# Two joint attention jobs side by side, and the attention's steps written out between the units of the projection

## What is computed

```
h = rmsnorm(x, norm_mix)
proj = h @ w_in                     # 1024 x 5888
qa, ka, va, qb, kb, vb, g_a, g_b = split(proj)
# a: 12 heads of 64 in three groups of four, windows (128,1), (512,4), (2048,16);
#    each head: softmax over its own window, with a slope times the distance
w_grp = softmax(stack(lses), axis=0)            # over the three groups
y_a   = sum(w_grp * outs)                       # 256 wide: four heads' sums over three groups
# b: 8 heads of 64, causal with a slope
merged = sigmoid(g_a) * (y_a @ w_up_a) + sigmoid(g_b) * (y_b @ w_up_b)
x = x + merged @ w_out
```

## Time and profile before

| | |
|---|---|
| median of 3 runs | 1197.73 us (1196.47 to 1199.54) |
| the profiled execution: its own time | 1196.15 us |
| its span, first to last instruction | 1194.3 us |
| PE busy | 1173.3 us (98% of the span) |
| PEld busy | 993.7 us (83%) |
| DVE busy | 810.8 us (68%) |
| ACT busy | 595.6 us (50%) |
| POOL busy | 51.1 us (4%) |
| TensorE's granted clock, mean | 0.999 |
| read from HBM | 251.63 MB, 212 GB/s over the span |

### The profile page before, as it was taken

The page is one execution under the profiler, slowest core; times in us unless marked ns, Lnnn a source line. Parts: engine busy times, 40 slices in busy tenths (PEclk is TensorE's granted clock), DMA queues, the critical chain, the costliest instruction groups (busy, mean ns, idle before and its releaser), DMA issues.

```text
span 1194.3 us, 15399 instructions
## 1 busy us (share of the span) xinstructions
PE 1173.3 (98%) x6300; PEld 993.7 (83%) x6300; DVE 810.8 (68%) x1037; ACT 595.6 (50%) x776; POOL 51.1 (4%) x101
## 2 busy tenths in 40 slices
PE   8999999999999999999999999999999999999998
PEld 6888887999999888888777888888789978888887
DVE  5777876437646658787899876787784657545544
ACT  8443346545563653433568554334465675533431
POOL 0011110000000001111000000111000000000000
PEclk9999999999999999999999999999999999999999
DMA  9888693553334668886725357887636405655540
GB/s 372 337 314 301 238 360 141 181 185 129 106 130 159 242 229 290 298 302 235 281 81 182 133 209 263 312 300 266 244 112 241 159 1 211 221 181 197 176 141 36
DMA packets 44422, 253.68 MB, mean 212 GB/s; under 512 B 5568, under 2 KB 5952, under 8 KB 20544
## 3 DMA queue, kind: packets, MB, share of 16 engines
q1 hardware_dynamic: 29088, 199.78, 46.1%
q0 software_dynamic: 13824, 50.34, 11.9%
q10 hardware_dynamic: 1440, 2.58, 0.6%
HBM read 251.63 MB, written 1.05 MB: 212 GB/s over the span
## 4 chain that ended last, share of the span: by engine, by line
PE 44%; ACT 2%; DVE 2%; DMA 1%; issue 1%; SPq 0%; DVEq 0%; ACTq 0%
PE ps L1767 11%; PE ps L1769 11%; PE ps L1768 11%; PE ps L1760 1%; PE ps L1762 1%; PE ps L1761 1%; DMA raw<-in_w 1%; ACT w_hi L449 1%; PE ps L1877 1%; PE ps L2141 1%; PE ps L2110 1%; PE ps L2267 0%; PE ps L1803 0%; DVE w_lo L1035 0%; PE ps L2124 0%
## 5 line engine op out<-in xcount | busy, mean ns | idle before, releaser
L1035 DVE TENSOR_TENSOR w_lo<-raw,w_hi 128x2048 fp32r<-128x2048 f32 x145 | 331.1, 2288 | 126.3 <-ACT w_hi L449 126.3
L449 ACT ACTIVATE w_hi<-raw 128x2048 fp32r<-128x2048 f32 x145 | 275.2, 1910 | 32.9 <-DMA raw<-in_w 32.7
L1767 PE MATMUL ps<-w_hi,h_hi_t 128*128 128x512 f32 (+1 forms) x720 | 286.5, 398 | 2.5 <-DVE h_lo_t L1386 1.1
L1769 PE MATMUL ps<-w_lo,h_hi_t 128*128 128x512 f32 (+1 forms) x720 | 277.9, 386 | 0.0
L1768 PE MATMUL ps<-w_hi,h_lo_t 128*128 128x512 f32 (+1 forms) x720 | 277.4, 385 | 0.0
L1767 PEld LDWEIGHTS ps<-w_hi,h_hi_t 128*128 128x128 f32 x720 | 135.4, 188 | 30.9 <-issue 3.5
L526 ACT ACTIVATE hid_hi<-ps 128x512 fp32r<-128x512 f32 (+1 forms) x48 | 27.0, 563 | 268.1 <-PE ps L1877 268.0
L1769 PEld LDWEIGHTS ps<-w_lo,h_hi_t 128*128 128x128 f32 x720 | 135.3, 188 | 28.0
L1768 PEld LDWEIGHTS ps<-w_hi,h_lo_t 128*128 128x128 f32 x720 | 135.6, 188 | 26.2 <-issue 1.4
L1760 PE MATMUL ps<-h_hi_t,w_hi 128*128 128x256 f32 x448 | 128.3, 286 | 1.3 <-DVE h_lo_t L1327 1.3
L1761 PE MATMUL ps<-h_lo_t,w_hi 128*128 128x256 f32 x448 | 126.7, 283 | 0.0
(11 more groups left out here) (219 smaller groups left out, 1616.2 us busy)
## 6 DMA issues: line engine op xcount, KB each, us to landing
raw<-in_w SPq DMA_DIRECT2D x146, 1024.0 KB, 4.9
ada_raw<-in_ada_w POOLq DMA_DIRECT2D x96, 512.0 KB, 5.2
raw_extra<-in_w SPq DMA_DIRECT2D x40, 1024.0 KB, 5.7
raw<-in_w SPq DMA_DIRECT2D x4, 256.0 KB, 5.9
gate<-in_ada_b ACTq DMA_DIRECT2D x2, 512.0 KB, 12.4
gate<-in_ada_b SPq DMA_DIRECT2D x2, 512.0 KB, 6.1
out_x<-x SPq DMA_DIRECT2D x4, 256.0 KB, 2.1
const<-in_const ACTq DMA_DIRECT2D x1, 768.0 KB, 7.9
```

The source lines that it names most:

```text
L449: act.activation(w_hi[SLOT[u]], raw[SLOT[u]], ACT.Copy).then_inc(hi_ready, 1)
L1035: V.tensor_tensor(w_lo[SLOT[u]], raw[SLOT[u]], w_hi[SLOT[u]].bitcast(F32), ALU.subtract) \
L1767: TE.matmul(dst, x_hi, wh, start=start, stop=False, skip_group_check=True)
L1769: return TE.matmul(dst, x_hi, wl, start=False, stop=last, skip_group_check=True)
```

## The change

Ten edits, all in the first attention and what stands around it:

1. `scores` and `pv` take two joint jobs, 0 with 1 and 2 with 3. Jobs 0 and 1 are heads (0, 4, 8) and (1, 5, 9), so in each pair one head lies in rows 0 to 63 and the other in rows 64 to 127. The matmuls are issued in turn, one of each job, into banks 2 to 4 and 5 to 7.
2. The sums of a joint job use 64 columns of the value tile for 64 rows of the output, one job in the lower half and one in the upper half of bank 1, issued in turn.
3. `turn` of jobs 1 and 3 goes to banks 5 to 7, that of 0 and 2 to banks 2 to 4, and `copy_probs` of jobs 1 and 3 goes into the buffer of `soft` that the job before has left.
4. `copy_y` copies both jobs of a pair at once.
5. The loops over n are gone: each engine's order is written out, with some steps between the two halves of a unit.
6. Units 11 to 21 sum in banks 0 and 1 instead of 0 alone.
7. On DVE the two `front` of a pair stand together, and `back` and `lo` behind them.
8. The gates of units 15 to 20 are copied plainly, and one sigmoid takes all twelve tiles; units 21 and 22 keep theirs.
9. y is split into tensors of its own, `y_hi_t` and `y_lo_t`, over the space of `soft`; the wait for unit 22 ahead of the split is gone, and the split stands ahead of the copy of unit 22.
10. The first units of `w_up` read these tensors.

On PE, the sums of the joint jobs. First the kernel before, between unit 13 and unit 14: the scores of job 3, the sums of job 0 and the turn of job 1 (`x3` is three equal instructions in a row).

The diff, cut to its core:

```diff
-W_IN_BANKS = [0, 1, 2, 3, 0, 1, 2, 0, 1, 2, 1] + [0] * 11 + [2]
+W_IN_BANKS = [0, 1, 2, 3, 0, 1, 2, 0, 1, 2, 1, 0, 1, 0, 0, 0, 1, 0, 0, 0, 0, 0, 2]
-SCORES, TURNED = 2, 5
-PV = ((1,), (1, 0))
+SCORES = [2, 5, 2, 5, 2, 2, 2, 2]
+TURNED = [2, 5, 2, 5, 5, 5, 5, 5]
+SUMS = 1
...
+        def prob_turned(j):
+            return soft[:, (j - 1) % 3, :, :] if j in (1, 3) else probT[:, :, :]
...
-            def split_hi(name, src, n, s, count):
-                act.wait_ge(s, count)
-                for c in range(n):
-                    act.activation(h_hi_t[:, y_tile(n, c), :], src(c), ACT.Copy).then_inc(h_hi, 1)
+            def split_y():
+                act.wait_ge(A[0]["out"], 8)
+                for c in range(6):
+                    act.activation(y_hi_t[:, c, :], qkv[:, c if c < 2 else 16 + c, :], ACT.Copy).then_inc(h_hi, 1)
...
+            for n in range(PASS, 12):
+                copy(n)
+            exps(0)
+            exps(1)
+            copy(12)
+            copy_probs(0)
+            copy(13)
+            copy_probs(1)
+            copy_y(0)
+            copy(14)
+            exps(2)
+            copy(15)
+            exps(3)
+            copy(16)
+            copy_probs(2)
...
+            copy(21, ACT.Sigmoid)
+            copy_probs(7)
+            copy_y(6)
+            act.wait_ge(proj_out, 21)
+            act.activation(qkv[:, 30:42, :], qkv[:, 30:42, :], ACT.Sigmoid).then_inc(gates_ready, 1)
+            copy_y(7)
+            split_y()
+            copy(22, ACT.Sigmoid)
...
 DVE
+            for n in range(11):
+                unit(n)
+            front(0)
+            front(1)
+            back(0)
+            unit(11)
+            back(1)
+            for n in range(12, 15):
+                unit(n)
+            front(2)
+            front(3)
+            back(2)
+            unit(15)
+            back(3)
...
 PE
+                def scores(*js):
...
+                    segs = [(SCORES[k] + s, *seg) for s in range(len(jobs[j][1])) for k in js for seg in jobs[k][1][s:s + 1]]
+                    for bank, q, kt, _, rows_, *_ in segs:
+                        TE.matmul(ps[:, bank, 0:P], qkv[rows_, q, 0:P], qkv[rows_, kt, 0:P], start=True,
...
+                def pv(*js):
+                    pe.wait_ge(a["copied"], js[-1] + 1)
...
+                    groups = [heads] if len(js) == 1 else [(heads[s], heads[3 + s]) for s in range(3)]
+                    for g, two in enumerate(groups):
+                        for probs, s, (_, _, v, _, _, rows_, _, _) in two:
+                            cols = slice(rows_.start, rows_.stop)
+                            TE.matmul(ps[rows_, SUMS, 0:T], qkv[:, v, cols], probs[:, s, 0:T], start=g == 0,
...
+            for n in range(PASS, 11):
+                unit(n)
+            unit(11, (0,))
+            scores(0, 1)
+            unit(11, (1,))
+            unit(12)
+            turn(0)
+            unit(13)
+            turn(1)
+            unit(14, (0,))
+            pv(0, 1)
+            unit(14, (1,))
+            scores(2, 3)
+            unit(15)
+            unit(16)
+            turn(2)
+            unit(17)
+            turn(3)
+            scores(4)
+            unit(18, (0,))
+            pv(2, 3)
+            unit(18, (1,))
+            scores(5)
+            turn(4)
+            unit(19)
+            scores(6)
+            turn(5)
+            pv(4)
+            unit(20)
+            scores(7)
+            turn(6)
+            pv(5)
+            unit(21)
+            turn(7)
+            pv(6)
+            unit(22, (0,))
+            pv(7)
+            unit(22, (1,))
```

More of the change, by code:

```diff
@@ L675, in copy_probs @@
                     act.wait_ge(a["turned"], j + 1)
-                    wait(act, a["pv"], j)
-                    act.activation(probT[:, 0:n, :], ps[:, TURNED:TURNED + n, 0:SEG], ACT.Copy) \
+                    wait(act, a["pv"], j - j % 2 if j < 4 else j)
+                    act.activation(prob_turned(j)[:, 0:n, :], ps[:, TURNED[j]:TURNED[j] + n, 0:SEG], ACT.Copy) \
                         .then_inc(a["copied"], 1)
                 def copy_y(j):
[L681 to L694, removed]
+                    count = 2 if j < 4 else 1
+                    act.wait_ge(a["pv"], j + count)
+                    act.activation(qkv[:, jobs[j][2], :], ps[:, SUMS, 0:T], ACT.Copy).then_inc(a["out"], count)
+                return exps, copy_probs, copy_y
             def stick():
@@ L997, in _, with copy @@
             hi(BASE["w_in"] + 7)
[L998 to L1002, removed]
-                    split_hi("y1", lambda c: qkv[:, c if c < 2 else 16 + c, :], 6, A[0]["out"], 8)
+            exps, copy_probs, copy_y = attention(0, attention_jobs_1())
+            def copy(n, function=ACT.Copy):
                 if n < W_IN_VALUES:
@@ L1731, in _, with unit @@
             front, back = attention(0, attention_jobs_1())
[L1732 to L1740 removed]
+            def unit(n):
+                lo(BASE["w_in"] + n + AHEAD)
+            for n in range(11):
[13 more added lines that the diff above has]
+            unit(16)
+            front(4)
+            unit(17)
+            back(4)
+            front(5)
+            unit(18)
+            back(5)
+            front(6)
+            unit(19)
+            back(6)
+            front(7)
+            unit(20)
+            back(7)
+            unit(21)
+            split_y()
+            unit(22)
             merge()
@@ L2061, in gqa @@
+                return scores, turn, pv
             def gqa():
@@ L2353, in _, with unit @@
             value_pass("w_in", 1)
-            step = attention(0, attention_jobs_1())
-            for n in range(PASS, 23):
-                before = max(m for m in range(n) if W_IN_BANKS[m] == W_IN_BANKS[n])
-                pe.wait_ge(proj_out, before + 1)
-                if n == 22:
-                    pe.wait_ge(A[0]["moved"], 8)
+            scores, turn, pv = attention(0, attention_jobs_1())
+            def unit(n, parts=(0, 1)):
+                if 0 in parts:
+                    pe.wait_ge(proj_out, max(m for m in range(n) if W_IN_BANKS[m] == W_IN_BANKS[n]) + 1)
+                    if n == 16:
+                        pe.wait_ge(A[0]["out"], 2)
+                    if n == 22:
+                        pe.wait_ge(A[0]["moved"], 8)
                 if n < W_IN_VALUES:
@@ L2373, in _ @@
                 if j < 2:
[L2374 to L2375 removed]
+                    rows_unit(u, 4 if j == 0 else 0, lambda k: y_hi_t[:, first + k, :],
+                              lambda k: y_lo_t[:, first + k, :], True, j == 0)
                     continue
```

125 lines of the change are left out of this document (58 added, 67 removed).

## The result

| | before | changed |
|---|---|---|
| median of 4 runs | 1197.68 us (1196.47 to 1199.54) | 1188.18 us (1187.18 to 1189.39) |
| ratio | | 0.992, 95% interval 0.9903 to 0.9937 |
| the profiled execution: its own time | 1196.15 us | 1187.38 us |
| its span | 1194.3 us | 1185.5 us |
| the stretch from unit 10 to `w_up` | 102.83 us | 94.16 us |

The change takes 0.8% off, 9.5 us between the medians and 8.8 us between the two profiled executions. The last row of the table is the measure used from here on. It begins 0.12 us behind the start of unit 10's last matmul and ends with the start of the first matmul of `w_up`: 368.91 - 266.08 before, 360.00 - 265.84 now. Nearly all of the gain lies in it (8.67 of 8.8 us), and nothing is given back later. It is also far steadier than a run's time: two runs of the changed kernel both gave 94.16, two of a later variant both 92.91.

A forecast was written before the change was run, and what follows sets the result against it. PE's own instructions were taken to set the time nearly everywhere. Gains of 9.13 us less costs of 1.48 gave 7.65 us off 1197.73, so 1190.1 us, 0.6% faster, with a range of 1187.0 to 1193.8.

The forecast's parts named there:

- scores of two pairs: Joint jobs' scores on PE, issued side by side: 2.58 us a pair instead of 4.32, a gain of 3.5 us.
- sums of two pairs: Joint jobs' sums over the values on PE, side by side: 2.40 us a pair instead of 4.12, gain 3.4 us.
- wait ahead of the first scores: PE's wait for ACT's copy of unit 10 goes, as half of unit 11 stands between: gain 0.75 us.
- wait at the end: Between unit 22 and `w_up`: the split of y need no longer wait for unit 22, gain 1.46 us.
- new wait at turn 0: PE waits ahead of turn 0 for probabilities delayed by ACT's longer queue: cost 1.1 us, bounds nothing to 1.7.
- more places: Attention work stands between units at 13 places instead of 11, 0.19 us each: cost 0.4 us.
- a pair takes 3 x 0.86: Scores of a joint pair priced as three times a two-head job's 0.86 us: 2.58 instead of 4.32.
- three such groups, 2.40: Sums of a joint pair priced as three two-head groups of 0.80 us: 2.40 instead of 4.12.
- The upper bounds: Largest gains given for the scores and sums side by side: 4.3 us for scores, 4.1 us for sums.
- third rival: No wait at turn 0, or pairs overlap better than by the rows: 1188.3 us, chance 13%.
- the slope of two rows: ACT's sigmoid at the end, from 1.50 us over 1536 values and `hi`'s 1.90 over 2048: 2.7 us for 3072.
- The rival that it might fall: Idle time at turn 0 drops PE's granted clock from 2.4 to 1.2 GHz: 1203 us, slower, chance 3%.

The follow-up runs named there:

- jobs apart: Changed kernel with unit matmuls between the two jobs' scores and between their sums in all four pairs, so nothing overlaps: 1197.85 us (1.0006), stretch 103.37.
- scores behind unit 10: Changed kernel with the scores of jobs 0 and 1 right behind unit 10, no half unit ahead of them: 1188.66 us in one run, stretch 94.91.
- own home of y alone: Kernel before, with only y split into tensors of its own and the split's wait for unit 22 removed: 1196.03 us beside 1198.23 (0.9987), stretch 101.36.
- table loaded early: Changed kernel with the exponential's table loaded by a one-value activation ahead of unit 11's copy: 1186.85 us (0.9911), again 1186.3 us (0.9913), stretch 92.91 both times.
- the run with more places: Changed kernel with unit parts inside each pair's scores and between its groups of sums, six stays more: 1190.13 us (0.9937), stretch 96.24.
- The two runs made for it: Changed kernel with six more stays, 1190.13 us (0.9937); changed kernel with early table load and two places fewer on PE, 1185.98 us (0.9913).
- the old banks: Changed kernel with units 11 to 21 all summing in bank 0 again: 1191.3 us (0.9946), stretch 97.80.
- another run: Changed kernel with only unit 16 moved back to bank 0: 1190.29 us in one run, stretch 96.31.

## Why the prediction was right, and where its terms were off

| term | predicted, us | measured, us | shown by |
|---|---|---|---|
| scores of two pairs | -3.48 | -4.32 (2 x (4.32 - 2.16)) | changed kernel; jobs apart |
| sums of two pairs | -3.44 | -4.04 (2 x (4.12 - 2.10)) | changed kernel; jobs apart |
| wait ahead of the first scores | -0.75 | -0.75 | scores behind unit 10 |
| wait at the end | -1.46 | -1.46 | own home of y alone, 1.47 |
| new wait at turn 0 | +1.1 | +1.21 | table loaded early, 1.25 |
| more places | +0.38 | +0.06 | count on both timelines |
| turns right ahead of scores or sums | not in the sum | +0.69 | count on both timelines |
| two-head jobs, units, rounding | 0 | -0.06 | the remainder |
| stretch | -7.65 | -8.67 | |

The forecast was 1190.1 us and the median is 1188.18, inside the range; the stretch, forecast as some 95 us, is 94.16. The sum is off by 1.02 us: 1.44 too little for the overlap, 0.48 too little for what is paid, and the remainder.

**The overlap** was the right mechanism, with a price too high for a pair of jobs. The terms "a pair takes 3 x 0.86" and "three such groups, 2.40" multiply a row that holds one stay in the divided array. The run with more places shows a group by itself at the same 0.80 us, and three in one stay at 2.10: 0.65 each, and 0.15 once. Scores go the same way, 0.86 for one and 2.16 for three: 0.65 each, and 0.21 once. That one job alone also takes 2.16 for three heads means that a second job in the other half adds nothing, as the records that start together show. The upper bounds that the prediction gave, 4.3 and 4.1, were the truth, and so was half of its third rival, pairs overlapping better than by the rows without the first start. That rival named 1188.3 us, without a working. That the median lies beside it is in part luck, since its other half, no wait at turn 0, didn't come. The Trainium skill (TensorEngine Tiling (Array Packing), Theoretical Speedup) allows up to twice the speed for a dimension of 64; I had weighed it with 8.4 us for both gains together and taken the rows instead. This trace agrees with it, at 8.36.

**The two old waits** came off at their size, each confirmed by a run of its own. At the end the sigmoid took 2.78 us where the slope of two rows had given 2.7, the split was on time, and the margin was 0.6 us instead of 0.35.

**Turn 0** was forecast from the length of ACT's queue. It waits for DVE's division as said, and the run with the early load shows its cause: the 1.28 us of the table load. Hidden, it gives back 1.25 us; ACT's 3.36 us of idle time ahead of a unit's copy had shown room for it.

**Places** were right in number and wrong in kind. I counted 0.19 us for each and two more of them. The two runs made for it agree with 0.19 outside and 0.15 inside, or 0.35 where a place also opens one more stay. But a turn between units starts the usual 0.12 behind the unit (287.58, 287.70 on the changed kernel's PE) and costs only 0.08 behind it. Counted through on both timelines, the eleven places cost 1.94 us in all and the thirteen 2.00.

What the sum had at nothing, without a reason, is the order inside a place. In the kernel before each turn stands last, right ahead of a unit; in the changed one four of the eight (turns 3, 5, 6 and 7) stand right ahead of scores or sums. PE's timeline, a joint job's turn first in the kernel before, then in the changed one:

```profile
297.30 0.36 PE L1760 MATMUL ps<-h_hi_t,w_hi 128*128 128x256 f32 x1
```

```profile
317.33 1.15 PE L2085 MATMUL ps<-const,soft 128*128 128x128 f32 x9
318.41 0.49 PE L2071 MATMUL ps<-qkv 64*128 64x128 f32 x4
```

From the turn's start (296.39 in the earlier trace rows) to what follows it takes 0.91 us before, and 1.08 here. For the two-head jobs it is 0.63 against 0.81 where scores stand ahead of the turn, and 0.58 against 0.75 where full-array work does. All eight turns take 6.15 us before and 6.84 now: the 0.69 of the table.

**The clock** stayed full, as forecast, with the 1.04 us idle at turn 0. The rival that it might fall had something to it: with the old banks it did, after a wait of 1.88 us, at a loss of 1.5. With the same wait in another run it didn't, and two of four executions of the first read a full clock as well.

**The rest of the way.** The medians differ by 9.5 us and the spans by 8.8. The 0.7 us between them are less than the wait at 987 us varies between executions, and no row of the stretch asks for more than 8.67.

## What to carry to other kernels

Look for matmuls that use half of the array's rows or columns and put the other half's work right beside them, in turn: here that halved 16.9 us of work at full overlap, and the other edits together brought 0.3 us, 2.21 of old waits removed against 1.96 for a new wait, turns and places. Keep such work in few, long stays, since each cost about 0.35 us here, with scores or with sums in it, put a full-array step such as a transpose behind them rather than right ahead of them or between two (0.17 to 0.18 us on the way in; counted here, not tried), and take a price per group from rows of two lengths, not from one row that has the stay's own cost in it. When a function's table load stands right behind a queue that others wait for, load it with a one-value activation in the engine's idle time before.

## What the runs showed of the hardware

- Two halves of the array in fp32 overlap completely: twelve pairs of records start within 0.01 us of each other, 0.107 us per record of 128 columns and 0.215 of 256, the same as for one half alone.
- They run as two streams that need not be issued in turn: with all 128-column blocks ahead of the 256-column ones and job ahead of job, a record of 256 columns started 0.11 us ahead of one of 128 that was issued before it, and a pair of scores took 2.70 us, not 4.32. The Trainium skill (TensorE: Matmul & The Clock Gate, Part 3: Packing small matmuls — row/col tiling) says that matmuls start and end in program order; with two halves in use, this trace shows starts out of it.
- Changing how the array is divided costs some 0.15 to 0.2 us inside a stay, from sums to scores as well as from a unit, and 0.19 outside; right behind a turn 0.17 to 0.18 on entry. The Trainium skill (TensorEngine Tiling (Array Packing), Key Properties) says that a change of mode drains the engine; the run with six more stays agrees that a change has a price, 0.35 us for each stay, while the drain itself shows in no view.
- The granted clock fell to its lower level for about 3.4 us behind a 1.88 us wait in one run, and not behind an equal wait in another; of four executions of the first, two read a mean of 0.998 and two of 1.000.
